# Blocks 1 to 5 of the first input projection as split fp32r products, with the weights' low halves made by Pool in place

## The reference, cut to what matters

```
proj = rmsnorm(h, norm_mix_even[i]) @ w_in_ab[i]
ssd_out = ssd_mixer(proj[..., :o0], proj[..., o0:o1], proj[..., o1:o2], ...)
attn_out = diff_attention(proj[..., o2:], ...)
h = h + jnp.concatenate([ssd_out, attn_out], axis=-1) @ w_out_ab[i]
```

## Time and profile before

| what | value |
|---|---|
| median of 3 runs | 1527.09 us (1522.82 to 1527.17) |
| profiled execution | 1525.42 us |
| its span in the trace | 1523.8 us |
| PE, PEld busy in the span | 1496.6 us (98%), 1214.2 us (80%) |
| DVE, ACT, POOL busy | 717.2 us (47%), 310.8 us (20%), 90.9 us (6%) |
| mean granted clock of TensorE | 0.987 |

### The profile page before, as it was taken

One profiled execution on the slowest core, in us unless ns is written; L12 is line 12 of the kernel. 1 busy time (PEld: TensorE's weight loads), 2 busy tenths in 40 slices (PEclk: granted clock), 3 DMA queues, 4 the chain that ended last, 5 costly groups with the idle time before them and its releaser, 6 DMA issues.

```text
span 1523.8 us, 45002 instructions
## 1 busy us (share of the span) xinstructions
PE 1496.6 (98%) x19964; PEld 1214.2 (80%) x19964; DVE 717.2 (47%) x1730; ACT 310.8 (20%) x498; POOL 90.9 (6%) x93
## 2 busy tenths in 40 slices
PE   8999999999999999999999999999999999999997
PEld 6776599999988887777777777778877777777785
DVE  5478456665488854322523533432523433433433
ACT  3375344443436502000000000000000000000002
POOL 0061000000034420000000000000000000000000
PEclk9999999999999999999999999999999999999998
DMA  9322055567423444999999999999999999999991
GB/s 287 114 83 82 3 165 166 168 207 224 147 83 111 139 167 178 394 393 391 393 392 390 386 389 392 381 391 390 385 390 388 387 387 390 388 384 391 387 387 59
DMA packets 221538, 431.60 MB, mean 283 GB/s; under 512 B 9546, under 2 KB 76624, under 8 KB 221040
## 3 DMA queue, kind: packets, MB, share of 16 engines
q1 hardware_dynamic: 218104, 425.34, 76.5%
q10 hardware_dynamic: 3256, 3.54, 0.7%
HBM read 427.80 MB, written 1.05 MB: 281 GB/s over the span
## 4 chain that ended last, share of the span: by engine, by line
PE 94%; DVE 4%; ACT 1%; issue 1%; DMA 0%; ACTq 0%; DVEq 0%
PE ps L1690 92%; PE ps L1707 1%; DVE arena L1084 1%; DVE ring_lo L1291 1%; DVE arena L1225 0%; DMA ktab<-in_k_table_dram 0%; ACT ring_hi L888 0%; DVE arena L1168 0%; DVE arena L1166 0%; ACT arena L701 0%; DVE arena L1193 0%; DVE arena L1199 0%; DVE xtk_lo L1508 0%; DVE arena L1194 0%; DVE arena L1200 0%
## 5 line engine op out<-in xcount | busy, mean ns | idle before, releaser
L1690 PE MATMUL ps<-raw,xg 128*32 128x384 f32 (+2 forms) x9216 | 525.6, 379 | 0.0
L1690 PEld LDWEIGHTS ps<-raw,xg 128*32 128x32 f32 x9216 | 390.6, 110 | 115.0 <-ACT xg L1009 0.2
L1558 DVE STREAM_TRANSPOSE ehT<-eh 32x96 f32<-32x96 f32 x896 | 241.7, 270 | 62.0 <-PE ps L1690 32.1
L1690 PE MATMUL ps<-raw,ehT 128*32 128x384 f32 (+2 forms) x4608 | 267.6, 379 | 0.0
L1546 DVE TENSOR_TENSOR eh<-esg,ps 128x384 f32<-128x384 f32 x56 | 31.1, 555 | 499.1 <-PE ps L1690 480.4
L1690 PEld LDWEIGHTS ps<-raw,ehT 128*32 128x32 f32 x4608 | 202.7, 110 | 49.7 <-issue 0.2
L1003 ACT ACTIVATE esg<-ps 128x384 f32<-128x384 f32 x56 | 27.3, 488 | 672.9 <-PE ps L1690 672.9
L1690 PE MATMUL ps<-xn_hi,ring_hi 128*128 128x272 f32 x544 | 160.8, 296 | 0.9 <-DVE ring_lo L1291 0.9
L1690 PE MATMUL ps<-xn_hi,ring_lo 128*128 128x272 f32 x544 | 158.7, 292 | 0.0
L1690 PE MATMUL ps<-xn_lo,ring_hi 128*128 128x272 f32 x544 | 158.0, 290 | 0.0
L1690 PE MATMUL ps<-xn,ring 128*128 128x272 f32 (+1 forms) x640 | 156.6, 405 | 0.9 <-DVE xn L1084 0.8
(11 more groups left out here) (299 smaller groups left out, 1187.4 us busy)
## 6 DMA issues: line engine op xcount, KB each, us to landing
raw<-in_moe_w_gate_dram SPq DMA_DIRECT2D x96, 1024.0 KB, 16.0
raw<-in_moe_w_up_dram SPq DMA_DIRECT2D x96, 1024.0 KB, 15.2
raw<-in_moe_w_down_dram SPq DMA_DIRECT2D x96, 1024.0 KB, 14.0
raw_ring<-in_moe_w_down_dram SPq DMA_DIRECT2D x16, 1024.0 KB, 14.2
raw_ring<-in_moe_w_gate_dram SPq DMA_DIRECT2D x16, 1024.0 KB, 15.7
raw_ring<-in_moe_w_up_dram SPq DMA_DIRECT2D x16, 1024.0 KB, 15.6
ring<-in_w_in_ab_dram SPq DMA_DIRECT2D x12, 1024.0 KB, 6.7
ring<-in_hy_w_in_dram SPq DMA_DIRECT2D x12, 1024.0 KB, 5.0
```

The costliest lines, as they stand in the source:

```text
L1558: V.transpose(ehT[GROUP * q:GROUP * q + GROUP, s % 2, g, :, :], src).then_inc(sem("ehT_ready"), 1)
L1690: return nc.tensor.matmul(o, l, r, start=start, stop=stop)
```

## The change: what it does

Blocks 1 to 5 of the projection are multiplied in split form, like the later ones. Block 0 stays in fp32.

- ScalarE copies the 8 tiles of `xn` to fp32r (`px_hi`), then block 1 (`first_high(1)`, into `pw_hi`, three buffers). In the loop over j it copies block j / 2 + 2 at every even j, ahead of that tile's own copy. For blocks 4 and 5 it waits for the end of the block that used the buffer.
- VectorE subtracts `px_hi` from `xn` (`px_lo`), after the norm and ahead of the parameters.
- Pool subtracts the high half from the block in the ring, in place (`ring_lo`), for n = 1 to 5, after its constants.
- TensorE waits for `px_low` and `first_low` and adds 48 fp32r matmuls in a block.
- To free semaphores, three are merged into others: `coef_ready` into `v_ready`, `squares3` into `squares2`, `xn3_ready` into `xn2_ready`, with the counts moved. They are cut below where they repeat.

```diff
+        px_lo = overlay("px_lo", 0, KT, T)
...
+        px_hi, pw_hi = overlay("px_hi", 13056, KT, T), overlay("pw_hi", 15232, 3, 256 * KT)
...
@@ gpsimd
             g(nc.gpsimd.memset(ind[:, 3:4], 1.0), sem("pool_consts"))
+
+            for n in range(1, 6):
+                pool.wait_ge(sem("first_high"), n)
+                g(nc.gpsimd.tensor_tensor(ring_lo[:, n % RING, 0:256 * KT], ring[:, n % RING, 0:256 * KT], pw_hi[:, n % 3, :].bitcast(F32), ALU.subtract),
+                  sem("first_low"))
             pool.wait_ge(sem("table_in"), 48)
...
-            pool.wait_ge(sem("coef_ready"), 1)
-            pool.wait_ge(sem("v_ready"), 1)
+            pool.wait_ge(sem("v_ready"), 2)
@@ scalar
+            for k in range(KT):
+                act.wait_ge(sem("xn1_ready"), k + 1)
+                nc.scalar.activation(px_hi[:, k, :], xn[:, k, :], ACT.Copy).then_inc(sem("px_high"), 1)
+
+            def first_high(n):
+                act.wait_ge(slot_in[n % RING], 16 * (n // RING + 1))
+                if n >= 4:
+                    act.wait_ge(sem("tile_ready"), NUMBER[("proj", 2 * (n - 3) + 1)] + 1)
+                nc.scalar.activation(pw_hi[:, n % 3, :], ring[:, n % RING, 0:256 * KT], ACT.Copy).then_inc(sem("first_high"), 1)
+
+            first_high(1)
             for j in range(8):
+                if j % 2 == 0:
+                    first_high(j // 2 + 2)
                 if j == 4:
...
-                        squares("down", "squares3", k)
+                        squares("down", "squares2", k)
@@ vector
             V.memset(crd[:, 7:8], 0.0).then_inc(used("ss1"), 1)
+            for k in range(KT):
+                dve.wait_ge(sem("px_high"), k + 1)
+                V.tensor_tensor(px_lo[:, k, :], xn[:, k, :], px_hi[:, k, :].bitcast(F32), ALU.subtract).then_inc(sem("px_low"), 1)
             dve.wait_ge(used("param"), 1)
...
-                        weighted_low(k, C_NMO, "xn3_ready", KT)
+                        weighted_low(k, C_NMO, "xn2_ready", KT)
...
@@ tensor
             for n in range(6):
-                linear("proj", 2 * n, n, xn, coming=sem("xn1_ready") if n == 0 else None)
+                if n == 0:
+                    linear("proj", 0, 0, xn, coming=sem("xn1_ready"))
+                else:
+                    pe.wait_ge(sem("px_low"), KT)
+                    pe.wait_ge(sem("first_low"), n)
+                    high, low = [a.rearrange("p (k n) -> p k n", k=KT) for a in (pw_hi[:, n % 3, :], ring_lo[:, n % RING, 0:256 * KT])]
+                    for j in range(2):
+                        o, c = open_tile("proj", 2 * n + j), slice(P * j, P * j + P)
+                        for k in range(KT):
+                            last = product(o[:, 0:T], high[:, k, c], low[:, k, c], (px_hi[:, k, :], px_lo[:, k, :]), k == 0, k == KT - 1)
+                        close(last)
                 if n == 0:
                     parameters()
...
-                    pe.wait_ge(sem("v_ready"), 3)
+                    pe.wait_ge(sem("v_ready"), 4)
```

More of the change, by code:

```diff
@@ L1422, in _ @@
                     v(V.reciprocal(invn, t[:, 0:8]), used("kn"))
-                    v(V.tensor_tensor(coefn, coef, invn.rearrange("p (k a) -> p k a", a=1).to_broadcast([P, KT, META]), ALU.mult), sem("coef_ready"))
+                    v(V.tensor_tensor(coefn, coef, invn.rearrange("p (k a) -> p k a", a=1).to_broadcast([P, KT, META]), ALU.mult), sem("v_ready"))
                 if m == 8:
@@ L1734, in add_squares @@
                 for k in range(k0, k0 + n):
-                    pe.wait_ge(sem(s), k + 1)
+                    pe.wait_ge(sem("squares2"), s + k + 1)
                     last = mm(o[:, 0:toks.stop - toks.start], ones[:], sq[:, k, toks], k == 0, k == KT - 1)
@@ L1943, in _ @@
                 out_columns(j, 1)
-            add_squares("ss2", "squares2", 0, 2)
+            add_squares("ss2", 0, 0, 2)
             linear("wo", 4, B_WO + 2, cat)
-            add_squares("ss2", "squares2", 2, 2)
+            add_squares("ss2", 0, 2, 2)
             linear("wo", 6, B_WO + 3, cat)
@@ L1969, in swiglu_columns @@
                             if first and c == 0 and part == 0 and j == 0 and k == KT - 1:
-                                add_squares("ss2", "squares2", 4, 4)
+                                add_squares("ss2", 0, 4, 4)
                                 pe.wait_ge(sem("xn2_ready"), KT)
@@ L1999, in _ @@
                 if b:
-                    add_squares("ss3", "squares3", 2 * b - 2, 2)
+                    add_squares("ss3", KT, 2 * b - 2, 2)
             pe.wait_ge(sem("sin_ready"), 3)
@@ L2042, in in_columns @@
                         if m == 0 and j == 0:
-                            pe.wait_ge(sem("xn3_ready"), k + 1)
+                            pe.wait_ge(sem("xn2_ready"), KT + k + 1)
                         c = slice(P * j, P * j + P)
@@ L2052, in _ @@
             for k in (6, 7):
-                pe.wait_ge(sem("squares3"), k + 1)
+                pe.wait_ge(sem("squares2"), KT + k + 1)
                 last = mm(o[:, 0:T], ones[:], sq[:, k, :], False, k == KT - 1)
```

## The result

The changed kernel takes **1553.18 us**, the median of 4 runs (1547.22 to 1553.76), against 1527.13 for the kernel before (4 runs, 1522.82 to 1527.26): a ratio of 1.0172, interval 1.0151 to 1.0193, 26 us slower. Its profiled execution took 1553.3 us, with a span of 1551.7 and a mean granted clock of 0.974 (0.987 before). Three of the four executions lie within 0.7 us of each other; the fourth, at 1547.22, has a granted clock of 0.979. 1548.3 was forecast, with a range of 1531 to 1556.

What follows compares the result with a forecast made beforehand. TensorE, with 94% of the chain of waits, was taken to bound the kernel, a second chain having 1.8 us of slack. 1525.4 (profiled execution) + 21.4 (last filter layer's shift) + 1.5 (clock) = 1548.3 us, range 1531 to 1556.

Steps and rivals of the forecast that it cites:

- TensorE's gain: Blocks 1 to 5 on TensorE: split products take 6.0 us for 7.5 each, 7.5 us if operands are there.
- High halves and W1: ScalarE makes W1's high half from 22.6 to 24.55; Pool's low half takes 4.8 us; block 1 starts at 29.4.
- Rival 3: Pool's in-place fp32r subtraction is slower, up to 8.7 us: +16 more, 1564 us; chance 0.07.
- W2 and what stands behind it: ScalarE waits for W2 until 30.8 ahead of tile 0's copy; parameters at 34.1, 9.6 us late against 1.8 slack.
- Rival 2: Not slower: TensorE paces the stage, W2 landing before 24.6; 1523.7 us, or 1518; chance 0.09.
- Pool against VectorE: VectorE instructions with two SBUF operands stand while Pool's runs; each low half costs VectorE up to 4.8 us.
- rival 1: Pool and VectorE do not hold each other, only ScalarE's W2 wait remains: +7.4 with clock, 1533 us; chance 0.10.
- Convolution 2 stands behind its first instruction: VectorE during Pool's W3 subtraction (45.4 to 50.2): convolution 2 is held after its first instruction and ends at 52.3.
- Exp, Ln and their tables 3.9 us: ScalarE's dt work after VectorE's dt maximum at 59.95: 3.9 us, so done at 63.85.
- Clock: TensorE's granted clock falls after standing 16 us before block 5: 1.5 us added, bounds 0 and 6.
- From the last filter layer on, every row later by the same amount: Sign of being right: behind the last filter layer the shift stays constant.
- if the shift grows behind 90 us: Sign of being wrong: rows behind 90 us come later by a growing amount.

Runs made afterwards that it cites:

- e7: Changed kernel plus 52 zero-column matmuls keeping TensorE occupied ahead of its wait for the first filter sine; 1550.5 us.
- e1: Changed kernel with ScalarE making W2's high half behind the copy of tile 0 and the parameters; 1547.5 us.
- e2: Changed kernel with Pool's five low halves left out, Pool writing zeros in their place and reading nothing; 1537.3 us.
- e11: Kernel before with only blocks 3 and 5 split, lows on VectorE, plus 8 zero-column matmuls ahead of the last filter layer; median 1527.4 us, ratio 1.0005.
- e12: Kernel before, nothing split, plus 8 zero-column matmuls on TensorE ahead of the last filter layer; median 1526.4 us, ratio 1.0012.
- e4: Changed kernel with W2's high half behind the parameters and Pool writing zeros instead of subtracting; 1529.1 us.
- e10: Changed kernel's split kept for blocks 3 and 5 only, highs placed where ScalarE stands anyway, low halves on Pool; 1529.7 us.

## Why the prediction was right

**TensorE's gain** (7.5 us in five blocks) is there at the full clock: e7's block 5 took 6.1 us. As the prediction said, blocks 1 to 4 are off the path. Block 5 is on it, and its 1.5 us did not arrive: at the lower clock it took 8.2 us, more than the 7.5 of an fp32 block.

**High halves and W1.** Forecast 22.6 to 24.55; measured 22.22 to 24.11. Pool's subtraction was put at 4.8 us; the five took 4.49 to 4.60. The two shapes of the earlier trace rows gave the slope rightly, and my allowance for passing waits was not needed: Pool, which began first each time, was not slowed. The floor of the Trainium skill ("GPSIMD Engine Reference", § 2.1), an estimate of 4.3, was 0.2 to 0.3 short. Rival 3 falls.

**W2 and what stands behind it.** Transfer 16.70 us for 16.5, landing 31.2 for 30.8, lambda products from 34.23 for 34.1, convolution 0 done at 41.7 for 41.65. e1 shows the price, 5.9 us at the last filter layer. Rival 2, which needed W2 early, falls.

**Pool against VectorE.** Named rightly as the main term: 11.6 us, by e2, and rival 1 falls with it. Even without Pool's reads e2's last layer came 10.6 us later than in the kernel before, where rival 1 has 5.9, or 7.4 with the clock. In detail one step was wrong and harmless: "Convolution 2 stands behind its first instruction". I took the one-operand TENSOR_SCALAR for free beside Pool and the taps for held; in fact the TENSOR_SCALAR itself was held (so no group of taps took the 6 to 7 us that the prediction named as a sign), at tiles 2 and 6. The group's end came out the same (52.5 for 52.3), since either waits for the same end of Pool's work.

**Two errors that in part cancelled, which is luck.** The dt terms were to return at 63.85 after "Exp, Ln and their tables 3.9 us"; VectorE waited only 2.18, and they were back at 61.9. ScalarE had loaded the Exp table at 54.98, ahead of its wait. So the sine ended at 80.5, not 82.5, 2.0 us early. From the sine to the start of the last filter layer it then took 9.5 us, where the forecast, with its 1.5 for the clock, has 8.15: 1.3 us late. TensorE stood 11.92 us, not 16, and part of the difference is clock: block 4 itself ran at a granted clock of 0.50 in 60 to 64 us and ended at 68.7 instead of 65.8, which cost nothing.

**Clock.** This is the mis-sized term: 1.5 us, with bounds of 0 to 6. It measured 2.5 before the last filter layer and, in the profiled execution, 5.7 behind it, 8.2 in all. In balance: the layer came 22.2 us later where 22.9 were forecast (21.4 and the 1.5), 0.7 less, and 5.7 more behind it make the 5.0 by which the profiled execution, 1553.3, exceeds 1548.3. The step "From the last filter layer on, every row later by the same amount" failed, and with it one of the prediction's own signs of being wrong came true, "if the shift grows behind 90 us". I had counted only what the clock costs after TensorE's standing before block 5, and taken the rest as equal in both kernels. The traces show that it also falls to 0.50 while TensorE is busy, behind stretches of small products (in the kernel before at 441 us, behind 32 products of 64x16), for 17 to 44 us in all between the last filter layer and the experts, and that the time of one kernel differs by 15 us with the clock. What decides how long it lasts was not settled. That the moment decides (e11, e12) is argued, not shown. Nor is it shown that the changed kernel must lose those 5.7 us: its execution at 1547.22 us is 6 us faster than the other three, and four are too few to say which is the rule. That the total still fell into the range owes something to the errors above.

**The merged semaphores** cost nothing visible: e4 and e10, which keep them, have stretches of 535.3 and 537.0 us beside the 535.7 of before, and the changed kernel's, without the clock's share, is 522.7 beside 523.8.

## What to carry to other kernels

Before work is given to an idle engine, ask what it reads, and when: here Pool's reads held VectorE, on the second-latest chain, for about 4 us at a time, which cost more than TensorE could save. Before a wait is added in front of an engine's queue, list what stands behind it and compare with that chain's slack, 1.8 us here against a stand of 7.1. And judge a gain of a few us both where it is made and at the end, there over many executions: the first tells whether the mechanism works, the second whether the clock left it there. One profiled execution each can't tell a change of 5 us from the 15 us by which one kernel differed from itself.

## What the runs showed of the hardware

- A TENSOR_SCALAR on one 128x272 fp32 tensor, which at 0.42 us takes about as long as a two-operand subtraction of that shape (the low halves of xn, 435 ns each), is still held by Pool: for 4.5 us by a Pool subtraction, up to 1.70 by a Pool memset. In the same places an instruction with two tensor operands is held by the subtraction and not by the memset. The time of such an instruction does not show whether it can be held.
- ScalarE can load a table ahead of the wait of the activation that needs it, and so hide 1.28 us. It did so for the Exp in the changed kernel, behind the added copy of a block. It did not for the first Silu (the load at 28.58 follows the wait of 3.67 us; in the changed kernel it is the one at 41.78, after 7.15), nor for the Exp in the kernel before (load at 37.24, after 3.01 us of waiting). What decides it was not tested. ScalarE in the changed kernel:

```profile
54.98 1.28 ACT L790 ACT_TABLE_LOAD   x1
...
59.74 0.22 ACT L790 ACTIVATE arena<-bcast 128x16 f32<-128x16 f32 x1 [3.47 <-DVE arena L1102]
```

- The time of unchanged work between 70 and 630 us varied by 12.7 us over these kernels (532.0 to 544.7) by the granted clock, at an engine that is busy nearly throughout (527.1 of 535.7 us in the kernel before); that is as much as three of Pool's holds. The Trainium skill, "TensorE: Matmul & The Clock Gate", § What's actually happening, puts what the clock's rise costs below 1% of a typical kernel. Half of the 17.1 to 44.4 us at 0.50 is 8.6 to 22.2 us, 0.6 to 1.4% of the kernel's time: 0.8% in the kernel before, which agrees, and 1.2% in the changed one, which does not.
